# A decoder layer with gathered experts: seven row slots instead of eight, and two constant tiles that stay in SBUF

## The reference, cut to what matters

```
def peer_ffn(hn, w_pq, sub_keys, u_experts, v_experts):
    q = (xt @ w_pq).reshape(T, PEER_HEADS, 2, PEER_QDIM // 2)
    s = jnp.einsum('thcd,hcnd->thcn', q, sub_keys)
    s_top, i_top = lax.top_k(s, PEER_TOPK)
    ...
    best_s, best_pos = lax.top_k(cand_s, PEER_TOPK)
    experts = jnp.take_along_axis(cand_i, best_pos, axis=-1)
    gates = jax.nn.softmax(best_s, axis=-1)
    ...
        u_sel = jnp.take(u_experts, eb, axis=0)
        a = jax.nn.gelu(jnp.einsum('td,thkd->thk', xb, u_sel)) * gb
        v_sel = jnp.take(v_experts, eb, axis=0)
        return jnp.einsum('thk,thkd->td', a, v_sel)
```

## Time and profile before

| | |
|---|---|
| median of 3 runs | 3350.63 us (3347.19 to 3352.07) |
| the profiled execution, its own time | 3343.47 us |
| its span (first to last instruction) | 3341.4 us |
| mean granted TensorE clock | 0.916 of full |
| busy share PE / DVE / ACT / POOL | 81% / 66% / 41% / 36% |
| DMA traffic | 1247.42 MB, of which the gathers 1073.81 MB |

### The profile page before, as it was taken

The page is one execution under the profiler, slowest core; times in us unless marked ns, Lnnn a source line. Parts: engine busy times, 40 slices in busy tenths (PEclk is TensorE's granted clock), DMA queues, the critical chain, the costliest instruction groups (busy, mean ns, idle before and its releaser), DMA issues.

```text
span 3341.4 us, 29096 instructions
## 1 busy us (share of the span) xinstructions
PE 2690.4 (81%) x8088; PEld 1449.8 (43%) x8088; DVE 2216.9 (66%) x4746; ACT 1367.4 (41%) x3681; POOL 1217.3 (36%) x1051
## 2 busy tenths in 40 slices
PE   8988889878988798788888798698889766666666
PEld 7665456443435364453344454463335222222222
DVE  2021277796775868886774868886775877777765
ACT  1122133585433343673543343683533343333333
POOL 0000033443433334344444334343343444444543
PEclk9987999979999899899999899899999898899988
DMA  6422399999999999999999999999999999999998
GB/s 249 155 80 98 129 396 368 404 383 415 427 420 402 405 427 425 372 413 412 422 424 419 387 403 406 347 371 408 419 410 393 427 427 427 427 426 414 425 427 346
DMA packets 187459, 1247.42 MB, mean 373 GB/s; under 512 B 22049, under 2 KB 31265, under 8 KB 41377
## 3 DMA queue, kind: packets, MB, share of 16 engines
q0 software_dynamic: 147456, 1073.81, 78.0%
q1 hardware_dynamic: 36384, 154.98, 11.9%
q10 hardware_dynamic: 3456, 16.78, 1.2%
HBM read 1224.77 MB, written 20.71 MB: 373 GB/s over the span
## 4 chain that ended last, share of the span: by engine, by line
PE 38%; DMA 36%; DVE 11%; ACT 6%; issue 4%; POOL 3%; DVEq 2%; ACTq 1%; SPq 0%; POOLq 0%
DMA rows<-in_experts,idx 30%; PE ps L942 14%; PE ps L975 8%; PE ps L961 7%; DVE rows L1340 3%; POOL rows L642 3%; DVE acc_v L1351 2%; DMA wbuf<-in_w_conv 2%; PE ps L1000 2%; ACT L802 1%; DMA wbuf<-in_w_o 1%; PE ps L928 1%; DMA wbuf<-in_w_ckvr 1%; PE ps L1013 1%; PE ps L1018 1%
## 5 line engine op out<-in xcount | busy, mean ns | idle before, releaser
L642 POOL DMA_INDIRECT rows<-in_experts,idx x1024 | 1213.6, 1185 | 2099.8 <-PE ps L942 1104.7
L942 PE MATMUL ps<-rows,diag 128*128 128x512 f32 x2952 | 1516.6, 652 | 366.2 <-ACT diag L695 338.2
L1340 DVE CUSTOM_DVE_ANT_0 rows<-rows,hn 128x1024 f32<-128x1024 f32 x1024 | 1236.9, 1224 | 648.0 <-DMA rows<-in_experts,idx 631.7
L942 PEld LDWEIGHTS ps<-rows,diag 128*128 128x128 f32 x2952 | 585.6, 208 | 1138.1 <-ACT diag L695 549.2
L684 ACT ACTIVATE gelu<-dots 128x1 f32<-128x1 f32 x1024 | 206.7, 202 | 1397.3 <-DVE dots L1340 1381.9
L975 PE MATMUL ps<-T,wbuf 128*128 128x256 f32 x1600 | 390.3, 395 | 67.3 <-DMA wbuf<-in_w_conv 33.4
L975 PEld LDWEIGHTS ps<-T,wbuf 128*128 128x128 f32 x1600 | 313.0, 198 | 170.4 <-issue 51.0
L961 PE MATMUL ps<-wbuf,T 128*128 128x512 f32 x768 | 361.6, 610 | 19.3 <-ACT T L850 8.7
L1351 DVE SCALAR_TENSOR_TENSOR acc_v<-rows,weight,acc_v 128x1024 f32<-128x1024 f32 x286 | 366.7, 1282 | 0.6 <-ACT weight L688 0.6
L688 ACT ACTIVATE weight<-gelu,gate 128x1 f32<-128x1 f32 x1024 | 301.8, 295 | 75.2 <-DVE gate L1319 3.6
L695 ACT ACTIVATE diag<-ident,weight 128x128 f32<-128x128 f32 x738 | 296.4, 402 | 65.8 <-PE ps L942 4.2
(11 more groups left out here) (201 smaller groups left out, 1835.2 us busy)
## 6 DMA issues: line engine op xcount, KB each, us to landing
wbuf<-in_w_conv SPq DMA_DIRECT2D x24, 1024.0 KB, 9.2
wbuf<-in_w_o SPq DMA_DIRECT2D x16, 1024.0 KB, 9.2
wbuf<-cross_a SPq DMA_DIRECT2D x16, 1024.0 KB, 9.3
wbuf<-cross_b SPq DMA_DIRECT2D x16, 1024.0 KB, 9.2
wbuf<-in_w_pq SPq DMA_DIRECT2D x16, 1024.0 KB, 9.3
rows<-in_experts,idx POOLq DMA_INDIRECT x1024, 12.5
wbuf<-in_w_cq SPq DMA_DIRECT2D x8, 768.0 KB, 9.3
wbuf<-in_w_ckvr SPq DMA_DIRECT2D x8, 576.0 KB, 8.7
```

What stands on the lines that cost most here:

```text
L642: pool.indirect_dma_start(out=rows[n % RR][:], out_offset=None, in_=w["experts"][:, :], in_offset=bass.IndirectOffsetOnAxis(ap=idx[:, b % ...
L942: mm = pe.matmul(ps[:, 6 + half, :], diag[:, m % DIAGS, :], rows[n % RR][:, D + half * HALFC:D + (half + 1) * HALFC], start=(k == 0), stop ...
L1340: dve.tensor_tensor_reduce(out=rows[n % RR][:, 0:D], in0=rows[n % RR][:, 0:D], in1=hn[:, b % 3, :], scale=1.0, scalar=0.0, op0=ALU.mult, o ...
```

## The change

- RR is 7 in place of 8: gather n now waits for the release of row n - 7.
- The eighth slot's 8 KB hold two tiles of 4 KB: `g_ffn` and the new `pkeys`, the keys of the choice. Each is loaded once, by SyncE, ahead of front 0, and stays.
- The keys are no chunk of the ring any more: a front has 32 chunks in place of 33, and pq0 to pq3 follow one another. TensorE reads `pkeys` in the `ps` stage, with the same matmuls.
- SyncE's wait for `oT` and its load of `g_ffn` in each front are gone. In their place there is one wait ahead of front 0, for the last reader of the fold chunk that lay in the same room (FOLD_LAST of chunk 11), and then the two loads.

```
-RR = 8
+RR = 7
...
-            + [(w["w_pq"], c, WCHUNK) for c in range(2)]
-            + [(w["keys"], 0, PHEADS * PKEYS)]
-            + [(w["w_pq"], c, WCHUNK) for c in range(2, 4)])
+            + [(w["w_pq"], c, WCHUNK) for c in range(4)])
...
-CHUNKS = 33
+CHUNKS = 32
...
-        last += [JOB[g, "pq", 1]] * 2 + [JOB[g, "ps", 4 * HB - 1]] + [JOB[g, "pq", 3]] * 2
+        last += [JOB[g, "pq", 1]] * 2 + [JOB[g, "pq", 3]] * 2
...
-        g_ffn = at("g_ffn_b", s0 + 20, [P, D])
...
         rows = [at(f"rows{s}", r0 + 8 * s, [P, 2 * D]) for s in range(RR)]
+
+        g_ffn = at("g_ffn_b", r0 + 8 * RR, [P, D])
+        pkeys = at("pkeys", r0 + 8 * RR + 4, [P, PHEADS * PKEYS])
...
                 loads(g, C_O, C_A)
-                filled(sp, g, "oT", HB - 1)
-                sp.dma_start(g_ffn[:], w["g_ffn"].to_broadcast([P, D])).then_inc(gffn_in, 16)
                 loads(g, C_A, CHUNKS)
...
+            sp.wait_ge(bank_set, FOLD_LAST[max(n for n in range(FOLD_CHUNKS) if n % FRING == FRING - 1)] + 1)
+            sp.dma_start(g_ffn[:], w["g_ffn"].to_broadcast([P, D])).then_inc(gffn_in, 16)
+            sp.dma_start(pkeys[:], w["keys"][0]).then_inc(pkeys_in, 16)
             for g in range(NG):
                 front(g)
...
-                        features(g, "pq", i, [(C_PQ + 3 * j, (2 * i + m) % 4 * P, HALFC) for m in range(2)],
+                        features(g, "pq", i, [(C_PQ + 2 * j, (2 * i + m) % 4 * P, HALFC) for m in range(2)],
...
-                        chunk_in(pe, chunk_no(g, C_KEYS))
+                        pe.wait_ge(pkeys_in, 16)
...
-                dve.wait_ge(gffn_in, 16 * (g + 1))
+                dve.wait_ge(gffn_in, 16)
```

More of the change, by code:

```diff
@@ L123, in block_chunks @@
             + [(w["cross_b"], c, WCHUNK) for c in range(4)]
-            + [(w["w_pq"], c, WCHUNK) for c in range(2)]
-            + [(w["keys"], 0, PHEADS * PKEYS)]
-            + [(w["w_pq"], c, WCHUNK) for c in range(2, 4)])
-C_CQ, C_CKVR, C_CONV, C_UQ, C_UKV, C_HEAD, C_O, C_A, C_B, C_PQ, C_KEYS = 0, 2, 4, 10, 12, 13, 16, 20, 24, 28, 30
-CHUNKS = 33
+            + [(w["w_pq"], c, WCHUNK) for c in range(4)])
+C_CQ, C_CKVR, C_CONV, C_UQ, C_UKV, C_HEAD, C_O, C_A, C_B, C_PQ = 0, 2, 4, 10, 12, 13, 16, 20, 24, 28
+CHUNKS = 32
 HRING = 4
@@ L395, in layer_kernel @@
         gffn_in = sem("gffn_in")
+        pkeys_in = sem("pkeys_in")
         mem_in = sem("mem_in")
@@ L1179, in front @@
                 emptied(pe, g, "nT", 2 * HB - 1)
-                keys = chunk(chunk_no(g, C_KEYS))
                 for j in range(2):
                     for i in (2 * j, 2 * j + 1):
-                        features(g, "pq", i, [(C_PQ + 3 * j, (2 * i + m) % 4 * P, HALFC) for m in range(2)],
+                        features(g, "pq", i, [(C_PQ + 2 * j, (2 * i + m) % 4 * P, HALFC) for m in range(2)],
                                  spaced(work, ROOMS[g]["pq"], 16))
                     if j == 0:
-                        chunk_in(pe, chunk_no(g, C_KEYS))
+                        pe.wait_ge(pkeys_in, 16)
                     for b in range(HB):
@@ L1194, in front @@
                                                T2[c * PDIM:(c + 1) * PDIM, hd, tokens(b)],
-                                               keys[c * PDIM:(c + 1) * PDIM, hd * PKEYS:(hd + 1) * PKEYS], start=True, stop=True)
+                                               pkeys[c * PDIM:(c + 1) * PDIM, hd * PKEYS:(hd + 1) * PKEYS], start=True, stop=True)
                                 if hd % 4 == 3:
```

## The result

The changed kernel takes 3387.33 us (median of 4 runs, 3377.39 to 3395.51) against 3351.35 us before. The ratio is 1.0108, 95% interval 1.0079 to 1.0138: 36 us slower, where +18.6 us was forecast; it lies inside the forecast's 3357 to 3400 us. The profiled execution took 3384.18 us, its span is 3382.1.

A forecast was written before the change was run, and what follows sets the result against it. The DMA engines were taken to bound everything after 430 us. 3343.5 + 30 (slot) - 7.4 (bytes) - 4 (ring) = 3362.1 us, +18.6; on the median 3350.6 that gives 3369 us, range 3340 to 3402.

The forecast's parts named there:

- Fewer bytes: Fronts 1 to 3 no longer load g_ffn and the keys while the DMA is full: 7.4 us less, bounds 0 and 7.4.
- the shorter ring: Ring of weights without the keys: TensorE waits less for pq in front 0, 4 us saved, at best 13, at least 0.
- The two loads and the wait ahead of front 0: SyncE's new wait and 1.05 MB of loads before front 0, where the DMA is mostly idle: cost 0, uncovered 2.5 us.
- TensorE's wait for pq: Expected sign in front 0: TensorE's wait for the pq chunks, 9.0 us before, would be near 5 us.
- The last stage: Rows alone: 4.2 gathers still queued last 10.3 us and cover its pauses; cost 0, at the most 18 us.
- The prediction's own sign of being wrong: Wrong if the fronts keep 405 GB/s or more with landings shortened, or the last stage falls below 416.
- Seven slots: One gather less queued makes dry spells in long pauses from 430 to 2610 us start sooner: 30 us, bounds 0 and 128.
- some 20: Expected sign: the fronts would be longer by some 20 us, at about 400 GB/s.
- The count of pauses: From 430 to 2610 us, 24 pauses over 8 us: 11 lose 2.46 us each, 13 lose half of it, 43 us.
- That discount: Slot term cut from 43 to 30 us, since TensorE, 84% busy in the fronts, would sometimes have been late anyway.
- Seven slots are enough: Rival: landing time falls with queue depth and the DMA never sees the missing slot; 3339 us, chance 0.18.
- The slots bind throughout: Rival: shorter pauses add up as the queue does not refill between them; 128 us, 3467 us; above 60 us chance 0.08.

The follow-up runs named there:

- eight slots in place: Kernel before with every tile in its old place, ring without the keys, no load of g_ffn or keys, other experts chosen: 0.9964 (0.9949 to 0.998).
- seven slots alone: Kernel before with RR 7 in place of 8 and nothing else, g_ffn and keys still loaded in each front: 1.0142 (1.0112 to 1.0172).
- The best version: Kernel before with keys kept, g_ffn loaded in each front, small tiles laid together, ring and rows at multiples of 256 bytes: 3340.33 us, 0.9962.
- the run with more bytes: Kernel before with seven slots, plus two unread loads of 1 MB more in each of fronts 1 to 3: 1.0179 (1.0152 to 1.0206).
- the limit from gather 740 on: Kernel before with its eight slots, but gathers from 740 on wait for the row seven before them: 0.999 (0.9972 to 1.0008).
- six slots: Changed kernel with RR 6 in place of 7, all else as in it: ratio to the kernel before 1.0669 (1.0642 to 1.0696).
- the three runs with odd places: Against the kernel before, rows at an odd multiple of 64 bytes: eight slots without reloads 1.0053, eight slots with kept keys 1.0054, rows shifted 64 bytes 1.0078.
- two runs: Kernel before with eight slots, shorter ring and small tiles moved: no g_ffn load and keys kept 1.0053; keys kept and g_ffn loaded in each front 1.0054.

## Why the prediction was right, and where its size was off

*Fewer bytes and the shorter ring, 7.4 + 4 us.* Right as a sum: 12 us measured with eight slots in place (7 to 17 by its interval), 11 us, give or take 14, as the changed kernel against seven slots alone. How it divides is less sure. The best version saves half the bytes (3.7 us, if a byte costs its full time, which the run with more bytes could not show) and still gains 13; its interval of plus or minus 5 us leaves the ring anything from about 4 to 14. In front 0 the ring's part is 2.6 us and not 4.3; in fronts 1 to 3 TensorE's waits for pq chunks, 8.7 us before, do not appear in the changed kernel's list; the sum had taken them at nothing.

*The two loads and the wait ahead of front 0, at nothing.* The timeline of SyncE's queue has them in the idle stretch, and front 0's first chunk at its old time (116.79 us):

```profile
102.89 0.33 SPq L597 DMA_DIRECT2D g_ffn_b<-in_g_ffn  x1
103.25 0.43 SPq L598 DMA_DIRECT2D pkeys<-in_keys  x1
116.62 1.13 SPq L524 DMA_DIRECT2D wbuf<-in_w_cq  x2
```

*TensorE's wait for pq, "near 5 us".* It was 6.43. The chunk came alone but for the store of h, issued right behind it; that the store held it up was not tried.

*The last stage, at 0.* Right within noise, shown by the limit from gather 740 on. The prediction's own sign of being wrong, less than 416 GB/s there, was met by 1 GB/s. From 2700 to 3300 us the changed kernel moves 422 GB/s where the kernel before moves 425, and the run with the limit there 422 as well. That is worth about 4 us of 600: a small loss is likely, and too small for these intervals.

*Seven slots, 30 us.* This is the term that was mis-sized: it measured 47 to 48 us, within its bounds of 0 and 128. Its mechanism, dry spells in the fronts' pauses, agrees with what was seen: the loss is in the fronts, where the DMA's idle time grew by about 40 us, the pause at 2542 us is drier, VectorE waits longer for rows. It is not the whole of it, since the gathers' packets took 18 us more as well. The fronts grew by 40 us and not by "some 20". The count of pauses had given 43 us, which both measurements allow and 30 they do not; the step that failed is the one behind it, "Some of this comes where TensorE (84% busy in the fronts) would have been late anyway, so I take 30 us". That discount had no row behind it, and no run showed one. That the count itself came out near is in part luck: it left out pauses below 8 us, charged those above 10 in full where the one at 2542 us lost 1.4 of 2.46, left the longer packets at nothing, and cannot be stretched to a second slot. For six slots the same thinking gave 60 to 100 us, and 188 were measured. Three things may stand behind this, and no run parts them. Queues that do not refill between pauses are what a count of single pauses leaves out. The same packets took 86 us more in all with six slots than with seven. And TensorE was slower: in the fronts its granted clock went from 0.93 to 0.92 and 0.90, and its busy time from 1651 to 1667 and 1717 us.

*The rivals.* "Seven slots are enough" describes the last stage within noise and the fronts not at all. The Trainium skill's fixed cost of about 2.0 us for a DMA (DMA: Bandwidth & Descriptors, section Anatomy of one DMA), which would have made it true, fits the shortest landing, 5.4 us here as well, and says nothing of how long a queue must last. "The slots bind throughout" came near one slot later: six slots starve both stages.

## What to carry to other kernels

A ring's depth is worth what its long pauses need, and not what its mean needs: read the median landing and the spacing of issues for the time that the queue lasts, and set that against the pauses between issues, stage by stage. A limit on the wait alone, over part of the program and with the buffers left in place, shows where a slot is missed without moving a byte. If a count of such pauses gives a price, discount it only for what a row shows.

## What the runs showed of the hardware

Where a large transfer lands in SBUF has a price. With the rows 64 bytes past a multiple of 512 the full DMA moved 421 GB/s and not 427, and the kernel was 0.78% slower (0.52% to 1.03%); with 256 bytes nothing changed (0.9998). The median 8 KB packet of the gathers took 312 ns in the three runs with odd places and 309 in the others, by the records of the traces. The Trainium skill (DMA: Bandwidth & Descriptors, section How a descriptor splits into AXI transactions) says that transactions start at multiples of 256 bytes and that a descriptor which does not start at one pays for beats it does not use. It tells this of reads; here the place written to was shifted, and the two shifts agree with the same rule for it. Places between 64 and 256 bytes were not tried. This small cost hid the savings in two runs and would have told the wrong story of them: by the expectations alone the shorter ring was to blame, until a stage in which it loads nothing was found to fall short as well.

Fewer rows on their way also cost something when the DMA is full. With a share of 1.01 from 2720 to 2920 us, the kernels with eight slots there and the rows at multiples of 256 bytes moved 426 or 427 GB/s, and those with seven 419 to 425 (the changed kernel 421), with a median packet of 309 ns in all of them. Why is not shown.
